# Allocating the small tensors ahead of the temporaries and the overlaid region in SBUF

## The reference, cut to what matters

```python
for l in range(2):                                     # first block
    x = x + 0.5 * swiglu(rmsnorm(x, norm_ffn1[l]), w_ffn1_in[l], w_ffn1_out[l])      # 1024 -> 2*2816 -> 1024
    h = rmsnorm(x, norm_mix[l])
    x = x + mixing_sublayer(h, w_in[l], ...)           # retention (4 heads) + forgetting attention (8 heads), gated
    x = x + 0.5 * swiglu(rmsnorm(x, norm_ffn2[l]), w_ffn2_in[l], w_ffn2_out[l])
x = rmsnorm(x, norm_final)
# second block: one layer
h = rmsnorm(x, g_mix);  proj = h @ w_in
# three gated branches: a gated linear recurrence, dilated attention with a bias by distance, attention to 256 memory rows
x = x + merged @ w_out
x = x + square(relu(rmsnorm(x, g_mlp) @ w_mlp_in)) @ w_mlp_out                       # 1024 -> 4096 -> 1024
return rmsnorm(x, g_final)
```

## Time and profile before

| | us |
|---|---|
| median of three executions | 3379.43 |
| the three executions | 3388.18, 3379.43, 3379.38 |
| the profiled execution's time | 3388.18 |
| its span, first to last instruction | 3386.4 |
| TensorE busy in it | 3285.5 (97%) |
| VectorE, ScalarE, GpSimd busy | 1520.5, 1113.9, 217.5 |

### The profile page before, as it was taken

How to read it: one execution, slowest core, us unless ns; L and a number is a source line. 1 busy time by engine, 2 the same in 40 slices (tenths; PEclk the granted TensorE clock), 3 DMA queues, 4 the chain that set the end, 5 groups by cost and what they waited for, 6 DMA issues and landing times.

```text
span 3386.4 us, 37236 instructions
## 1 busy us (share of the span) xinstructions
PE 3285.5 (97%) x15068; PEld 2680.0 (79%) x15068; DVE 1520.5 (45%) x2397; ACT 1113.9 (33%) x1570; POOL 217.5 (6%) x165
## 2 busy tenths in 40 slices
PE   8999899999999999999999999999999779999997
PEld 6888787778888888888777888888896558788886
DVE  5434444445434444344445555345432443455353
ACT  4222244333322332233443233233223552332221
POOL 1000101002000000001110010002000000110001
PEclk9999999999999999999999999999998889999999
DMA  4222521122222232223111232223222112223231
GB/s 133 98 95 94 150 71 57 57 87 94 100 96 97 94 100 94 99 90 117 57 57 63 94 109 96 95 95 97 94 77 68 56 58 91 96 93 100 93 100 69
DMA packets 91550, 303.09 MB, mean 90 GB/s; under 512 B 10228, under 2 KB 16500, under 8 KB 90832
## 3 DMA queue, kind: packets, MB, share of 16 engines
q1 hardware_dynamic: 91380, 300.71, 27.2%
HBM read 298.52 MB, written 5.29 MB: 90 GB/s over the span
## 4 chain that ended last, share of the span: by engine, by line
PE 90%; DVE 4%; issue 3%; ACT 2%; DMA 1%; SPq 0%; POOL 0%; DVEq 0%; POOLq 0%; ACTq 0%
PE bank L1302 81%; PE out_ps L1189 1%; PE score_ps L1166 1%; PE turn_ps L1177 1%; PE score_ps L1221 1%; PE turn_ps L1136 1%; PE out_ps L1234 1%; ACT w_hi L1330 1%; PE score_ps L1168 0%; DVE w_lo L1670 0%; PE score_ps L1198 0%; PE out_ps L1208 0%; DMA raw<-w_mix 0%; PE turn_ps L1115 0%; PE score_ps L1265 0%
## 5 line engine op out<-in xcount | busy, mean ns | idle before, releaser
L1670 DVE TENSOR_TENSOR w_lo<-raw,w_hi 128x1024 fp32r<-128x1024 f32 (+1 forms) x548 | 672.2, 1227 | 1285.2 <-ACT w_hi L1330 1284.5
L1302 PE MATMUL bank<-in_hi,w_hi 128*128 128x512 f32 x2672 | 1070.1, 400 | 17.8 <-DVE in_lo L1676 11.9
L1302 PE MATMUL bank<-in_hi,w_lo 128*128 128x512 f32 x2672 | 1045.2, 391 | 0.0
L1302 PE MATMUL bank<-in_lo,w_hi 128*128 128x512 f32 x2672 | 1045.0, 391 | 0.0
L1330 ACT ACTIVATE w_hi<-raw 128x1024 fp32r<-128x1024 f32 (+1 forms) x548 | 569.1, 1039 | 1243.5 <-PE bank L1302 1222.0
L1302 PEld LDWEIGHTS bank<-in_hi,w_hi 128*128 128x128 f32 x2672 | 505.8, 189 | 131.7 <-issue 20.2
L1302 PEld LDWEIGHTS bank<-in_hi,w_lo 128*128 128x128 f32 x2672 | 504.4, 189 | 107.6
L1302 PEld LDWEIGHTS bank<-in_lo,w_hi 128*128 128x128 f32 x2672 | 505.6, 189 | 103.1 <-issue 3.7
L1302 PE MATMUL bank<-hid_hi,w_hi 128*128 128x512 f32 x960 | 373.4, 389 | 0.0
L1302 PE MATMUL bank<-hid_lo,w_hi 128*128 128x512 f32 x960 | 373.4, 389 | 0.0
L1302 PE MATMUL bank<-hid_hi,w_lo 128*128 128x512 f32 x960 | 373.4, 389 | 0.0
(11 more groups left out here) (253 smaller groups left out, 2942.2 us busy)
## 6 DMA issues: line engine op xcount, KB each, us to landing
raw<-w_ffn_in SPq DMA_DIRECT2D x176, 512.0 KB, 3.4
raw<-w_mix SPq DMA_DIRECT2D x90, 512.0 KB, 3.4
raw<-w_ffn_out SPq DMA_DIRECT2D x80, 512.0 KB, 3.4
raw<-w_mixb SPq DMA_DIRECT2D x58, 512.0 KB, 3.4
raw<-w_mlp_in SPq DMA_DIRECT2D x32, 512.0 KB, 3.4
raw<-w_mlp_out SPq DMA_DIRECT2D x32, 512.0 KB, 3.4
raw<-w_w_out SPq DMA_DIRECT2D x16, 512.0 KB, 3.4
raw<-w_ffn_out SPq DMA_DIRECT2D x16, 256.0 KB, 2.7
```

The lines of the kernel that those rows point to most:

```text
L1302: mm = pe.matmul(ps, lhs, rhs, start=first and step == 0, stop=last and step == 2, skip_group_check=True)
L1670: dve.tensor_tensor(w_lo[:, i % SPLIT, 0:cols], raw[:, i % RAW, 0:cols], w_hi[:, i % SPLIT, 0:cols].bitcast(F32), ALU.subtract).then_inc(S ...
```

## The change

Three edits, all in the allocation of SBUF at the head of `build`. The calls that allocate `tmp` and the overlaid region `m` move behind those of the small tensors. `halfb` is allocated with 32 columns in place of 24, a multiple of the new constant `LINE` (16 words, 64 bytes), and a view of its first 24 columns is used in its place. No instruction, transfer, wait, shape or order of work is edited.

```diff
+LINE = 16
...
         w_hi, w_lo = sb("w_hi", [P, SPLIT, UNIT], F32R), sb("w_lo", [P, SPLIT, UNIT], F32R)
-        tmp_sb = sb("tmp", [P, NTMP, S])
-
-        f, r = F32, F32R
-        m = overlay(
...
         vec = sb("vec", [P, NVEC])
         ident, ones, ident_r = sb("ident", [P, P]), sb("ones", [P, P]), sb("ident_r", [P, P], F32R)
...
         table_sb = sb("rel_table", [P, 3 * GH])
-        halfb = sb("halfb", [P, 3 * DT])
+        halfb = sb("halfb", [P, LINE * ((3 * DT + LINE - 1) // LINE)])[:, 0:3 * DT]
+        tmp_sb = sb("tmp", [P, NTMP, S])
+
+        f, r = F32, F32R
+        m = overlay(
...
```

More of the change, by code:

```diff
@@ L907, in build @@
         w_hi, w_lo = sb("w_hi", [P, SPLIT, UNIT], F32R), sb("w_lo", [P, SPLIT, UNIT], F32R)
+        vec = sb("vec", [P, NVEC])
+        ident, ones, ident_r = sb("ident", [P, P]), sb("ones", [P, P]), sb("ident_r", [P, P], F32R)
+        small = overlay([("ssum", [P, S], F32), ("tri", [P, P], F32)],
+                        [("forget_parts", [P, S], F32R), ("tri_r", [P, P], F32R)])
+        rstd_sb, ssum_sb, tri, tri_r = sb("rstd_b", [P, S]), small["ssum"], small["tri"], small["tri_r"]
+        forget_parts = small["forget_parts"]
+        stat_sb = sb("stat", [P, 8, 8])
+        soft_sb = sb("soft", [P, 4, 4])
+        col_sb = sb("col", [P, 3, 8])
+        lruv = sb("lruv", [P, 11, DT])
+        table_sb = sb("rel_table", [P, 3 * GH])
+        halfb = sb("halfb", [P, LINE * ((3 * DT + LINE - 1) // LINE)])[:, 0:3 * DT]
         tmp_sb = sb("tmp", [P, NTMP, S])
```

## The result

The kernel became slower: 3407.16 us (3406.69 to 3408.14) against 3379.40, a ratio of 1.0077 with a 95% interval of 1.0061 to 1.0093, or 27.8 us between the medians. The forecast was no change, within 3371 to 3390.

The account below looks back on a forecast made before the run. TensorE, busy 97% of the span with 90% of the chain, was taken to bound the kernel. All terms were 0, within 5.8 us either way, so the forecast stayed at 3379.4 us, range 3371 to 3390.

Parts of the forecast that it names:

- two small terms: VectorE's 4% and ScalarE's 2% of the chain, and awaited transfers: each 0, bounds 1.8 us and 1.5 us.
- TensorE on moved tiles. Term: 0.: Line 1302's 4,128 matmuls reading moved tiles would stream at the same 226 ns pitch, adding 0.
- bound of 2.5 us: Limit either way for matmuls on moved tiles: 4,128 x 226 ns = 933 us, by 1/376.
- the doubt left: Reservation behind the 0.88 for no change: distances between operands that no pair before has.
- The evidence from starts 4, 8 and 12 bytes off: VectorE's shifted accesses to `pad` took 684 and 750 to 752 ns, like unshifted ones (682, 752): odd starts cost nothing.
- the first one: Faster: matmuls on moved tiles lose 13 ns of overhead each, 54 us, to 3326 us; chance 0.05.
- The rival for slower: VectorE operations on moved tiles stretch as two read streams collide: 41 us, to 3420 us; chance 0.07.
- The 1.30 of that rival: Stretch seen in `mrg_lo_a`, 896 for 689 ns, applied to VectorE's 135 us of the chain to give 41 us.
- VectorE, ScalarE, transfers: VectorE and ScalarE operations on moved tiles and table transfers such as `decay`: each 0, bounds 1.8 and 1.5 us.
- The estimate of 0.2 us: Possible saving on the 15.1 us `decay` transfer: 4 beats of 260 per 8,192-byte row, if writes follow the read price.

Follow-up runs that it names:

- line64: The full change with LINE = 64 words in place of 16, so `halfb` has 64 columns; timed against the kernel before: 3380.69 us, ratio 1.0004.

## Why the prediction was wrong

**The path.** Right: TensorE bounds the kernel, and the time would move only if matmuls streamed at another rate, or through two small terms. They did, and 4,128 matmuls by 6.6 ns are 27.2 of the 27.8 us.

**The step that failed is "TensorE on moved tiles. Term: 0."** Its bound of 2.5 us was a tenth of what came. I took `in` and `hid` for "different distances to the weights", and `dil_hi_t` for a test at another offset. By the very addresses that I had worked out, none was different in the way that counts: `xT` to `w_lo`, `tmp` and `m` all start at 128 modulo 256, tiles are 2,048 bytes and `dil_hi_t` is 1,024 off, all multiples of 256. The trace of before held thousands of matmuls at one value of the deciding variable. That they agreed to the nanosecond said nothing about another value. The change moved it to the value that I even named ("from 128 to 0 modulo 256"), and I did not ask which row had such a pair. What the runs showed in place of 0 is 6.6 ns for each of the 4,128 matmuls at a distance of 128. I did write that the doubt left was "a property of distances between operands that no pair before has"; that was it, but as a loss I priced it on VectorE alone, with a chance of 0.07.

**The evidence from starts 4, 8 and 12 bytes off** was from VectorE, reading `pad`. It held for VectorE, and I carried it over to TensorE. There a distance of 4 bytes has the longest pitch of all that were measured with fp32r (237.5 ns).

**The rivals.** The mechanism was in the first one, with its sign turned: I asked whether the 13 ns between 213 and 226 came from the position of the moving operand relative to the weights and might be lost. The position does set part of the pitch, but before stood already at the best of all distances tried. The rival for slower had the wrong engine: VectorE's instructions kept their durations (683/688/695), and its stretch on `mrg_lo_a` stayed with GpSimd's moment, as argued. The 1.30 of that rival was a mean of two kinds: of its eight executions before, four took 1,098 to 1,107 ns and four 693 or 694.

**VectorE, ScalarE, transfers.** Right. `decay` landed in 14.7 us instead of 15.1, and the wait behind it was 15.6 instead of 17.1, both once. The estimate of 0.2 us, from the price that the Trainium skill gives (DMA: Bandwidth & Descriptors, section How a descriptor splits into AXI transactions), can't be told from such a spread.

**The ports.** I leaned on the rule that only the port shared by VectorE and GpSimd is contended (the Trainium skill, SBUF — State Buffer, section Who interferes with whom). For these two engines the trace agrees: after the change too, the four executions of `mrg_lo_a` that overlap an addition of GpSimd to `gate` take 1,107 ns, and the four that overlap none 692 or 693. The same section gives TensorE two read ports, one for the moving operand and one for the weights, and calls them independent. In time the two operands aren't independent here: with the same shapes and the same number of weight loads, and nothing else running, the pitch is 226.7 ns at the best distance and 229.0 to 237.5 at the others. The measurement decides; whether it is the ports that are at work, no run shows. The section also says that "PE and ACT never wait on anyone"; in the runs of matmuls alone nothing else was at work, so they don't test that.

No layout tried beats before. line64 keeps the order of the change and costs nothing (1.0004).

## What to carry to other kernels

Where TensorE streams fp32r tiles of 512 columns with a fresh load of 128 columns of weights for each, keep the moving tiles and the weights a multiple of 256 bytes apart: it was worth 0.8% here for a third of the large matmuls and 1.3% for the other two thirds. Round up whatever lies between them, not to a line of 64 bytes but to 256. For other widths measure first: with 448 and 256 columns a distance of 64 was better, and no type but fp32r and plain fp32 was measured. Compare like with like by counting matmuls in a steady window rather than by the median duration. And before taking equal durations on many tiles as proof that addresses don't matter, work out the addresses and see whether any two tiles differ in the way that the change makes them differ.

## What the runs showed that I had not expected

An unused tensor of 128 bytes costs 25 us of 3380 in a kernel in which no instruction changes. The effect has a period of 256 bytes and a second, smaller dip at 64 (229.1 ns). At 256 columns it is the other way round (119.9 ns at 0 against 118.7 at 128), and in plain fp32 there is none (429.2 at all four distances). At the best distance the matmuls of 512 columns run in an even pitch of 226.7 ns. At a distance of 128 they alternate between about 238 and 229, or fall into a longer cycle with a mean of 232.4: the same layout gave both.
